# Prompt attention of a hybrid encoder step: the order of the query tiles, their score banks, and the engine that adds the bias

## The reference

```
def diff_attention(q, k, v, qpos, kpos, lam, rel_bias):
    s = jnp.einsum('bqhmd,bkhmd->bhmqk', q, k, preferred_element_type=jnp.float32) * (DA_DK ** -0.5)
    bias = rel_bias[rel_bucket(kpos[None, :] - qpos[:, None])].astype(jnp.float32)
    ...
    visible = (kpos[None, :] // CHUNK) <= (qpos[:, None] // CHUNK)
    p = jax.nn.softmax(jnp.where(visible, s + bias, -jnp.inf), axis=-1)
    attn = p[:, :, 0] - lam * p[:, :, 1]
    return jnp.einsum('bhqk,bkhd->bqhd', attn.astype(v.dtype), v)
```

## Time and profile before

| | us |
|---|---|
| median of 3 runs | 1875.02 |
| lowest, highest | 1866.8, 1877.81 |
| the profiled execution | 1872.0 |
| its span, first to last instruction | 1870.2 |
| prompt attention in it, first scores to last output copy | 589.26 to 730.17 |

### The profile page before, as it was taken

The page is one execution under the profiler, slowest core; times in us unless marked ns, Lnnn a source line. Parts: engine busy times, 40 slices in busy tenths (PEclk is TensorE's granted clock), DMA queues, the critical chain, the costliest instruction groups (busy, mean ns, idle before and its releaser), DMA issues. The chain is left out here.

```text
span 1870.2 us, 23797 instructions
## 1 busy us (share of the span) xinstructions
PE 1651.3 (88%) x9399; PEld 1463.5 (78%) x9399; DVE 986.2 (53%) x1686; ACT 629.7 (34%) x1137; POOL 443.5 (24%) x270
## 2 busy tenths in 40 slices
PE   4489998779997886758977999999999999999896
PEld 2378987659996664646767999999988988989775
DVE  1665515860003665443345666666656677667744
ACT  1422222202111563343233222222344445444532
POOL 0331111113220000016544333333361111111132
PEclk8789999979997999988988999999999999999998
DMA  8544110112223001614561222212236334444442
GB/s 278 193 149 169 36 34 3 46 48 62 53 77 130 1 1 46 226 34 123 190 233 48 68 62 64 68 57 78 81 113 180 115 113 148 129 161 124 143 154 72
DMA packets 164564, 192.27 MB, mean 103 GB/s; under 512 B 7858, under 2 KB 126875, under 8 KB 164416
## 3 DMA queue, kind: packets, MB, share of 16 engines
q1 hardware_dynamic: 139626, 132.11, 22.9%
q10 hardware_dynamic: 19612, 40.93, 6.8%
q0 software_dynamic: 5216, 17.71, 2.7%
HBM read 173.62 MB, written 17.11 MB: 102 GB/s over the span
## 5 line engine op out<-in xcount | busy, mean ns | idle before, releaser
L564 PE MATMUL PS<-h_hi,weights_hi 128*128 128x384 f32 x1280 | 436.6, 341 | 10.5 <-POOL h_lo L2125 5.9
L2112 POOL TENSOR_TENSOR weights_lo<-weights_raw,weights_hi 128x1024 fp32r<-128x1024 f32 x99 | 253.2, 2559 | 766.6 <-ACT weights_hi L1690 742.6
L565 PE MATMUL PS<-h_lo,weights_hi 128*128 128x384 f32 x1280 | 433.9, 339 | 0.0
L566 PE MATMUL PS<-h_hi,weights_lo 128*128 128x384 f32 x1280 | 433.6, 339 | 0.0
L1690 ACT ACTIVATE weights_hi<-weights_raw 128x1024 fp32r<-128x1024 f32 x202 | 213.8, 1059 | 216.9 <-PE PS L1015 104.7
L564 PEld LDWEIGHTS PS<-h_hi,weights_hi 128*128 128x128 f32 x1280 | 243.9, 191 | 17.4 <-issue 12.7
L565 PEld LDWEIGHTS PS<-h_lo,weights_hi 128*128 128x128 f32 x1280 | 244.0, 191 | 0.0
L566 PEld LDWEIGHTS PS<-h_hi,weights_lo 128*128 128x128 f32 x1280 | 243.6, 190 | 0.0
L1013 PE MATMUL PS<-weights_hi,g_hi 128*128 128x512 f32 x396 | 160.6, 405 | 15.2 <-DVE weights_lo L1637 12.9
L2240 POOL TENSOR_TENSOR g_lo<-g_T,g_hi 128x384 fp32r<-128x384 f32 x66 | 81.6, 1237 | 372.3 <-ACT g_hi L2007 372.3
L1014 PE MATMUL PS<-weights_lo,g_hi 128*128 128x512 f32 x396 | 158.6, 401 | 0.0
(11 more groups left out here) (365 smaller groups left out, 2506.4 us busy)
## 6 DMA issues: line engine op xcount, KB each, us to landing
weights_raw<-in_w_up_dram SPq DMA_DIRECT2D x88, 512.0 KB, 4.0
weights_raw<-in_w_down_dram SPq DMA_DIRECT2D x66, 512.0 KB, 4.4
w_ada_unit<-in_w_ada_dram SPq DMA_DIRECT2D x32, 512.0 KB, 5.4
weights_raw<-in_w_in_dram SPq DMA_DIRECT2D x24, 512.0 KB, 4.2
weights_raw<-in_w_out_dram SPq DMA_DIRECT2D x24, 512.0 KB, 4.1
w_ada<-in_w_ada_dram SPq DMA_DIRECT2D x4, 2048.0 KB, 16.1
k_cache<-in_cache_k_dram ACTq DMA_DIRECT2D x8, 1024.0 KB, 5.8
x_scratch<-x_new POOLq DMA_DIRECT2D x9, 512.0 KB, 6.3
```

Of the source, the lines that this page charges most:

```text
L564: pe.matmul(out, wh, xh, start=(i == 0), stop=False)
L565: pe.matmul(out, wh, xl, start=False, stop=False)
L566: mm = pe.matmul(out, wl, xh, start=False, stop=(i == n - 1))
L2112: mark(gp.tensor_tensor(WL[n % 3][:, :], WR[:, n % 3, :], WH[n % 3][:, :].bitcast(F32), ALU.subtract), "w_lo")
```

## The change

The tiles of a head are taken in the order 7, 0, 6, 1, 5, 2, 4, 3: a long tile (i of 4 or more, two banks a map) and a short one (one bank a map) in turn. Long tiles have banks 0 to 3, short ones banks 4 and 5. `scores(s)` now waits for both exponentials of s-2, the tile before it of the same kind, in place of the first exponential of s-1. The identity products go; VectorE adds the bias to the scores in PSUM, 256 columns (128 for tile 0) for each map, ahead of the maximum, and waits for its own result in between. `BH`, `BL`, `IDR` and the three instructions that filled them go too. The turned bias goes to banks 5 to 7, and TensorE waits for `bias_ready` only before the second tile's scores.

```
+        TILE_ORDER = [7, 0, 6, 1, 5, 2, 4, 3]
+        def score_bank(i, m):
+            return 2 * m if i >= 4 else 4 + m
...
-            pe.wait_ge(*once("bias_ready"))
-            blocks = [(h, i) for h in range(NH) for i in range(NPT)]
+            blocks = [(h, i) for h in range(NH) for i in TILE_ORDER]
...
-                if s >= 1:
-                    pe.wait_ge(sem("exp"), 2 * s - 1)
-                S = [2 * ((2 * s + m) % 3) for m in range(2)]
+                if s >= 2:
+                    pe.wait_ge(sem("exp"), 2 * (s - 1))
+                if s == 1:
+                    pe.wait_ge(*once("bias_ready"))
+                S = [score_bank(i, m) for m in range(2)]
...
-                for m in range(2):
-                    cuts = sorted({lo, min(W, (lo // 512 + 1) * 512), W})
-                    for b0, b1 in zip(cuts, cuts[1:]):
-                        out = PS[:, S[m] + b0 // 512, b0 % 512:b0 % 512 + b1 - b0]
-                        pe.matmul(out, IDR[:, :], BH[:, h, 2 * P - W + b0:2 * P - W + b1], start=False, stop=False)
-                        mm = pe.matmul(out, IDR[:, :], BL[:, h, 2 * P - W + b0:2 * P - W + b1], start=False, stop=True)
-                    mm.then_inc(sem("scores"), 1)
...
-                        c0 = 1024 * ((2 * s + m) % 3)
-                        mark(ve.tensor_reduce(MX[:, 2 * (s % 2) + m:2 * (s % 2) + m + 1], PSF[:, c0:c0 + W], AX.X,
+                        c0 = 512 * score_bank(i, m)
+                        S = PSF[:, c0:c0 + W]
+                        lo = max(0, W - 2 * P)
+                        ch(ve.tensor_tensor(S[:, lo:W], S[:, lo:W], BIASP[:, h, 2 * P - (W - lo):2 * P], ALU.add))
+                        mark(ve.tensor_reduce(MX[:, 2 * (s % 2) + m:2 * (s % 2) + m + 1], S, AX.X,
```

More of the change, by code:

```diff
@@ L215, in build @@
     TMPA = r("kv_tmp_a", [P, T])
-    BH = at("bias_hi", [P, NH, 256], tmpa_off, F32R)
-    BL = at("bias_lo", [P, NH, 256], xr_off + 4096, F32R)
+    BIASP = at("bias_prompt", [P, NH, 256], tmpa_off)
     BIASS = at("bias_sample", [P, 144], tmpa_off + 4096)
@@ L234, in build @@
     ATB = [r("attn_T_a", [P, D])]
-    IDR = r("ident_r", [P, P], F32R)
-    BIASP = at("bias_prompt", [P, NH, 256], R1)
     ATB.append(at("attn_T_b", [P, D], xr_off))
@@ L443, in build @@
         LATE_SECTIONS = [2, 5, 3, 4]
-        PIECES = [sum(1 + (u % NPT >= 4) for u in range(t)) for t in range(NH * NPT + 1)]
+        TILE_ORDER = [7, 0, 6, 1, 5, 2, 4, 3]
+        def score_bank(i, m):
+            return 2 * m if i >= 4 else 4 + m
+        PIECES = [sum(1 + (TILE_ORDER[u % NPT] >= 4) for u in range(t)) for t in range(NH * NPT + 1)]
         PAIRS_AT_NORM = [2, 4, 6, 8]
@@ L784, in _ @@
             for h in range(NH):
-                pe.matmul(PS[:, h // 2, (h % 2) * 256:(h % 2 + 1) * 256], C("flip"),
+                pe.matmul(PS[:, 6 + h // 2, (h % 2) * 256:(h % 2 + 1) * 256], C("flip"),
                           BREV3[:, h, :] if h < 3 else BREV1[:, :], start=True, stop=True)
-            pe.matmul(PS[:, 2, 0:144], C("flip16"), BREVS[:, :], start=True, stop=True)\
+            pe.matmul(PS[:, 5, 0:144], C("flip16"), BREVS[:, :], start=True, stop=True)\
               .then_inc(sem("pe_once"), 1)
-            pe.wait_ge(*once("bias_ready"))
-            blocks = [(h, i) for h in range(NH) for i in range(NPT)]
+            blocks = [(h, i) for h in range(NH) for i in TILE_ORDER]
             NBK = len(blocks)
@@ L797, in scores @@
                 W = (i + 1) * P
-                lo = max(0, W - 2 * P)
-                if s >= 1:
-                    pe.wait_ge(sem("exp"), 2 * s - 1)
-                S = [2 * ((2 * s + m) % 3) for m in range(2)]
+                if s >= 2:
[3 more added lines that the diff above has]
+                S = [score_bank(i, m) for m in range(2)]
                 for c0 in range(0, W, 512):
@@ L804, in scores @@
                     for m in range(2):
-                        pe.matmul(PS[:, S[m] + c0 // 512, 0:c1 - c0], QT[m * DK:(m + 1) * DK, h, i * P:(i + 1) * P],
-                                  KTT[m * DK:(m + 1) * DK, h, c0:c1], start=True, stop=c1 <= lo)
-                for m in range(2):
-                    cuts = sorted({lo, min(W, (lo // 512 + 1) * 512), W})
-                    for b0, b1 in zip(cuts, cuts[1:]):
-                        out = PS[:, S[m] + b0 // 512, b0 % 512:b0 % 512 + b1 - b0]
-                        pe.matmul(out, IDR[:, :], BH[:, h, 2 * P - W + b0:2 * P - W + b1], start=False, stop=False)
-                        mm = pe.matmul(out, IDR[:, :], BL[:, h, 2 * P - W + b0:2 * P - W + b1], start=False, stop=True)
-                    mm.then_inc(sem("scores"), 1)
+                        mm = pe.matmul(PS[:, S[m] + c0 // 512, 0:c1 - c0], QT[m * DK:(m + 1) * DK, h, i * P:(i + 1) * P],
+                                       KTT[m * DK:(m + 1) * DK, h, c0:c1], start=True, stop=True)
+                        if c1 == W:
+                            mm.then_inc(sem("scores"), 1)
             def attn_turn(t, piece):
@@ L906, in _ @@
                     h, j = divmod(4 * i + q, NT)
-                    row = h * NPT + j if j < NPT else NH * NPT
+                    row = h * NPT + TILE_ORDER.index(j) if j < NPT else NH * NPT
                     mm = pe.matmul(PS[:, i % 2, q * P:(q + 1) * P], EL[:, row:row + 1].to_broadcast([P, P]), ident,
@@ L1322, in _ @@
             ve.wait_ge(*once("bias_turned"))
[L1323 to L1330, removed]
+            mark(ve.tensor_copy(BIASP[:, 0:2, :], PS[:, 6, :].rearrange("p (h n) -> p h n", h=2)), "dve_step")
+            mark(ve.tensor_copy(BIASS[:, :], PS[:, 5, 0:144]), "dve_step")
+            ch(ve.tensor_copy(BIASP[:, 2:4, :], PS[:, 7, :].rearrange("p (h n) -> p h n", h=2)))
+            out(ve.tensor_tensor(BIASP[:, :, P:2 * P], BIASP[:, :, P:2 * P],
+                                 C("future").unsqueeze(1).to_broadcast([P, NH, P]), ALU.add), "dve_once")
             PSF = PS[:, :, :].rearrange("p b n -> p (b n)")
-            blocks = [(h, i) for h in range(NH) for i in range(NPT)]
+            blocks = [(h, i) for h in range(NH) for i in TILE_ORDER]
             NBK = len(blocks)
@@ L1843, in _ @@
             PSF = PS[:, :, :].rearrange("p b n -> p (b n)")
-            blocks = [(h, i) for h in range(NH) for i in range(NPT)]
+            blocks = [(h, i) for h in range(NH) for i in TILE_ORDER]
             NBK = len(blocks)
             def exps(s, m):
-                W, q = (blocks[s][1] + 1) * P, s % 2
+                i, q = blocks[s][1], s % 2
+                W, c0 = (i + 1) * P, 512 * score_bank(i, m)
                 if s >= 2:
```

## The result

| | us |
|---|---|
| before, median of 20 runs | 1869.99 |
| after, median of 20 runs | 1877.34 (1871.39 to 1881.12) |
| ratio after/before | 1.0031, 95% interval 1.002 to 1.0042 |
| span of the profiled execution, before and after | 1870.2, 1874.7 |
| the stage, end of the bias products to the last output copy, before | 584.75 to 730.17 = 145.4 |

The changed kernel is 0.31% slower by the ratio, about 5.8 us; the two medians differ by 7.4 us, 0.39%, which is still inside the interval. That is inside the half per cent that was called no change, but the twenty runs show it. The stage grew by 4.7 us in the profiled executions and the span by 4.5. What lies ahead of the stage took 2.35 us less and what lies behind it 2.1 us more; the two nearly cancel, and the stage holds the difference.

A forecast was written before the change was run, and what follows sets the result against it. The prediction took a serial ring through VectorE, ScalarE's copy and TensorE as the bound, 32.6 us a head. -8.4 us at full clock plus +9 for the clock gave +0.6, 1872.6 us, put at 1876 for the median; range 1863 to 1890.

The forecast's parts named there:

- Beginning, ring and end, -8.4 us: Stage at full clock: beginning -3.0, first head -3.0, middle heads +0.8, last head +0.4, end -3.6 us.
- the walk: Tracing the new order through the engines' queues, long tile to long tile; gave 32.6 us a head, before 32.2.
- The rule on a lower price of the add: VectorE's bias add, taken as 433 ns: at the skill's 424 or 392 ns the sum would be 0.3 or 1.3 us lower.
- The clock, +9 us: TensorE's pauses drop its clock to 1.2 GHz: first head +3 to 4.5 us, three other heads 4.5 in all.
- the ring: Serial path between long tiles: adds, maxima, second exponential, copy of second piece, transpose, products, scores; 32.6 us a head.
- (1): Rival: VectorE becomes the bound in the loop, 28 us a head, about 1858 us; chance 0.12.
- (2): Rival: pauses keep half or more of the loop at 1.2 GHz, +12 to +14 us, 1888 us; chance 0.25.
- (3): Rival: pauses don't drop the clock in the loop, only part of the first head is slow; -5, 1870 us; chance 0.18.

The follow-up runs named there:

- fill_pauses: Changed kernel with scores of short tiles 0 to 3 multiplied 8, 3, 1, 1 times more on TensorE, extras thrown away; ratio 0.9951 to before, stage 137.9 us.
- adds_twice_filled: fill_pauses with each bias add on VectorE made twice; ratio 1.007 to the kernel before.
- later_filled_less: Changed kernel with transposes, copies and products one step later, short tiles' scores multiplied 4, 2, 1, 0 times more; ratio 0.9918 to before, median 1857.00 us.
- bias_on_tensor: Changed kernel with its order, banks and waits, but bias added by identity products on TensorE again; ratio 0.9936 to before, stage 134.3 us.
- fill_short_scores: Changed kernel with every short tile's scores multiplied twice, the first pair thrown away; ratio 0.9995 to before, stage 148.3 us.
- order_alone: Kernel before with only the new order of tiles, old banks, waits and identity products; ratio 1.0008 to before, stage 144.4 us.

## Why the prediction was right, and where it wasn't

**The forecast of no large gain held.** 1876 was named, 1877.34 measured. But the closeness is luck. It was built on 1872.6 for the profiled execution plus 3.0 to the median of three runs; with twenty runs the median of before is 1869.99, below the profiled execution, so the base was 5 us too high. The change itself was forecast at +1 us and measured at +5.8 by the ratio, so it was some 5 us too low. The two errors cancel.

**Beginning, ring and end, -8.4 us: the mechanism was right, and the sum is close.** fill_pauses, nearly the changed kernel at full clock, has a stage 7.5 us shorter than before, with 8.6 us at 1.2 GHz left in it. In its parts: until the first maximum -2.7 us (for -3.0, which was the early end of the forecast's own 2.1 to 3.0), first head -1.5 (for -3.0, and it holds the stretch of 6.8 us at 1.2 GHz), middle heads +0.6 (for +0.8), the last head and the end -3.9 (for -3.2). A head was 32.5 us for 32.6, the pairs 8.43 for 8.47 (tile 7 to 6), and 4.25 + 3.50 = 7.75 for 7.78 from tile 4 to 7 in the third head. The add took 0.43 us for 0.433, and adds_twice_filled put it where the walk had it, in both maps of the long tiles.

**The rule on a lower price of the add.** The figures of the Trainium skill (VectorE: DVE Perf Modes, the section on the TRN2 errata) were 424 ns for an fp32 tensor_tensor and 392 by the table's VectorE entry for PSUM to SBUF. Measured were 0.42 to 0.43 us: the first agrees. The second is 8% low here, for an add that also reads SBUF and writes to PSUM.

**The clock, +9 us: mis-sized.** Its mechanism was right and its size wasn't. In the first head the forecast pause of 4.5 us was 4.46 us, and 13.7 us at 1.2 GHz followed in three stretches, for 10 to 15. In each later head it took one drop of 3.4 to 7 us; there were three, two and one in heads 2 to 4, each of 3.4 us (20 us, where 10 to 21 had been allowed). So the time at 1.2 GHz, 34 us behind pauses, lay in the forecast's range; its price was wrong. The forecast took 0.30 of such a stretch as lost, TensorE's average share of the ring. Measured: 1.6 of 3.4 us, or 12.2 us for 27 us more of low clock than in fill_pauses, 0.45. In the six drops of heads 2 to 4 the low stretch begins from 0.1 us before the end of a pause to 0.7 us behind it, just where the ring runs through TensorE: transposes, products and scores, one after the other. With 0.45 and these 27 us the term is 12, and the change +4. An estimate, not measured: if the 6.8 us that fill_pauses keeps in its first head cost 0.45 too, the clock's term is 15 and the sum without it -10.6.

**The rivals.** (1), VectorE as the bound, did not come with this change, but it is what remains once copy, transpose and products leave the ring: 29.4 us a head in later_filled_less. (2), most of the loop at half clock, needed 59 us; the stage had 36, 34 of them behind pauses. It was its mechanism, not its size. (3), the pauses without their drops, is nearly what fill_pauses shows: 1861 rather than 1870, of which 5 us are the base that was too high.

## What to carry to other kernels

Before moving work off an engine that has the ring's longest pauses, ask what else that work may do: here 144 small products on TensorE became 64 adds on VectorE, and with the same order, banks and waits the stage grew by 15.8 us, 12.2 of them by the clock. Walk a ring through every in-order queue, and look for a small instruction of one tile that stands behind a large one of another; moving one copy between two exponentials gave 6.4 us. And price a clock drop where it lands on the path, not by the engine's mean share.

## What the hardware showed that was not expected

- Useless matrix products made the kernel faster: an estimated 4.5 us of them a head took 12.2 us off the stage, with a granted clock of 1.00 in place of 0.90 in the last heads.
- In the changed kernel TensorE was busy 75 of 101 us and its clock fell six times, each time for 3.4 us; in bias_on_tensor, busy 82.6 of 91.7 us, it never fell in the same heads. fill_short_scores, busy 79.8 of 99.9, was no better than the changed kernel, while fill_pauses, busy 79.6 of 92.8, held it. So the mean load doesn't tell where the clock falls.
- A single pause doesn't tell it either. The pause before the drop at 662.7 was 2.90 us, that of the earlier trace rows 2.92; one head later the same 2.90 us brought no drop. In adds_twice_filled the same three pauses, of 1.9 to 2.0 us, came in each of heads 2 and 3, with one drop in the first of them and none in the second. order_alone had two drops with no pause over 0.92 us ahead of them, and fill_pauses none with waits of up to 1.1 us, the last number here (from 600 to 715 us):

```profile
PE PS L511 <- ACT attn_T_a L1864: 15.4, 22, 1.1
```

Long pauses made drops frequent: six in three heads with pauses of up to 2.9 us, none or two in the kernels whose pauses there stay under 1.3. What decides a single drop stays open.
